# Hybrid decoder trunk: issue order of the rounded-weight and remainder products within a K tile

## What is computed

```python
def swiglu(h, w_gate, w_up, w_down):
    return (jax.nn.silu(h @ w_gate) * (h @ w_up)) @ w_down

for l in range(DEPTH):                       # DEPTH = 2
    x = x + 0.5 * swiglu(rmsnorm(x, norm_ffn1_g[l]), ffn1_w_gate[l], ffn1_w_up[l], ffn1_w_down[l])
    h = rmsnorm(x, norm_mix_g[l])
    proj = h @ w_in[l]
    q, k, v, c_b, c_c, c_u, g_attn, g_conv = jnp.split(proj, split_idx, axis=-1)
    ...
    merged = jax.nn.sigmoid(g_attn) * y_attn + jax.nn.sigmoid(g_conv) * y_conv
    x = x + merged @ w_out[l]
    x = x + 0.5 * swiglu(rmsnorm(x, norm_ffn2_g[l]), ffn2_w_gate[l], ffn2_w_up[l], ffn2_w_down[l])
return rmsnorm(x, final_g)
```

## Time and profile before

| what | value |
|---|---|
| median of three runs | 1123.29 us |
| lowest and highest | 1123.13 and 1127.27 us |
| the profiled execution's span | 1122.4 us |
| mean granted TensorE clock | 0.993 |

### The profile page before, as it was taken

How to read it: one execution, slowest core, us unless ns; L and a number is a source line. 1 busy time by engine, 2 the same in 40 slices (tenths; PEclk the granted TensorE clock), 3 DMA queues, 4 the chain that set the end, 5 groups by cost and what they waited for, 6 DMA issues and landing times.

```text
span 1122.4 us, 19933 instructions
## 1 busy us (share of the span) xinstructions
PE 1099.8 (98%) x6512; PEld 967.6 (86%) x6512; DVE 830.8 (74%) x1016; ACT 642.9 (57%) x908; POOL 20.2 (2%) x38
## 2 busy tenths in 40 slices
PE   6999999999999999999899999999999999999996
PEld 5888888888899888888788888888888998888885
DVE  5877767778898877666667776767788988676666
ACT  7655544556765655554455555445667656555454
POOL 5100000000000000000000000000000000000000
PEclk9999999999999999999989999999999999999998
DMA  8766655655555565655645656465445655656551
GB/s 218 244 188 186 196 172 177 215 163 161 170 188 170 176 198 182 192 171 176 205 133 181 202 171 194 158 209 188 150 154 183 196 175 179 195 176 199 171 188 37
DMA packets 202462, 201.76 MB, mean 180 GB/s; under 512 B 7904, under 2 KB 201472, under 8 KB 202416
## 3 DMA queue, kind: packets, MB, share of 16 engines
q1 hardware_dynamic: 200288, 199.25, 56.6%
q0 software_dynamic: 992, 1.87, 0.8%
q10 hardware_dynamic: 1136, 0.05, 0.1%
HBM read 199.32 MB, written 1.84 MB: 179 GB/s over the span
## 4 chain that ended last, share of the span: by engine, by line
PE 96%; DVE 1%; ACT 1%; DMA 1%; issue 1%; SPq 0%; DVEq 0%; ACTq 0%
PE acc L1114 57%; PE acc L1121 31%; PE acc L1118 4%; DMA raw<-in_ffn_w_gate_dram 1%; PE mixed L1118 1%; PE score L1118 1%; PE mixed L1154 0%; PE score L1222 0%; ACT w_hi L474 0%; PE mixed L1121 0%; PE score L1121 0%; PE mixed L1243 0%; PE mixed L1230 0%; PE mixed L1236 0%; ACT L508 0%
## 5 line engine op out<-in xcount | busy, mean ns | idle before, releaser
L1114 PE MATMUL acc<-xm,w_hi 128*128 128x512 f32 x2048 | 727.9, 400 | 6.9 <-issue 4.3
L1121 PE MATMUL acc<-xm,w_lo 128*128 128x256 f32 x2048 | 575.2, 281 | 0.0
L758 DVE TENSOR_TENSOR w_lo<-raw,w_hi 128x1024 fp32r<-128x1024 f32 (+1 forms) x387 | 455.6, 1199 | 147.7 <-ACT w_hi L474 146.7
L1114 PEld LDWEIGHTS acc<-xm,w_hi 128*128 128x128 f32 x2048 | 386.4, 189 | 100.9 <-issue 7.7
L474 ACT CAST w_hi<-raw 128x1024 fp32r<-128x1024 f32 (+1 forms) x387 | 389.6, 1030 | 132.7 <-PE acc L1121 120.6
L1121 PEld LDWEIGHTS acc<-xm,w_lo 128*128 128x128 f32 x2048 | 388.3, 190 | 0.2
L1121 PE MATMUL acc<-hm,w_lo 128*128 128x256 f32 x896 | 251.4, 281 | 0.0
L1114 PE MATMUL acc<-hm,w_hi 128*128 128x512 f32 x704 | 247.8, 397 | 0.0
L1121 PEld LDWEIGHTS acc<-hm,w_lo 128*128 128x128 f32 x896 | 169.7, 189 | 0.0
L486 ACT COPY acc_lo<-acc 128x512 f32<-128x512 f32 x144 | 84.2, 585 | 134.9 <-PE acc L1121 134.7
L1114 PEld LDWEIGHTS acc<-hm,w_hi 128*128 128x128 f32 x704 | 132.2, 188 | 32.3
(11 more groups left out here) (145 smaller groups left out, 476.7 us busy)
## 6 DMA issues: line engine op xcount, KB each, us to landing
raw<-in_ffn_w_gate_dram SPq DMA_DIRECT2D x88, 512.0 KB, 4.8
raw<-in_ffn_w_up_dram SPq DMA_DIRECT2D x88, 512.0 KB, 3.8
raw<-in_ffn_w_down_dram SPq DMA_DIRECT2D x80, 512.0 KB, 4.6
raw<-in_w_in_dram SPq DMA_DIRECT2D x80, 512.0 KB, 4.3
raw<-in_w_out_dram SPq DMA_DIRECT2D x16, 512.0 KB, 4.1
raw<-in_ffn_w_down_dram SPq DMA_DIRECT2D x16, 256.0 KB, 3.1
raw<-in_w_branch_attn_dram SPq DMA_DIRECT2D x8, 512.0 KB, 3.5
raw<-in_w_branch_conv_dram SPq DMA_DIRECT2D x8, 512.0 KB, 3.9
```

Of the source, the lines that this page charges most:

```text
L758: nc.vector.tensor_tensor(w_lo[:, s, 0:tiles, :], raw[:, s, 0:tiles, :], w_hi[:, s, 0:tiles, :], ALU.subtract).then_inc(lo_split, 1)
L1114: nc.tensor.matmul(banks[:, m, :], w_hi[:, r, k, cols], x[:, 0:2 * SEQ], start=first and k == 0, stop=False, skip_group_check=True)
L1121: mm = nc.tensor.matmul(banks[:, m, 0:SEQ], w_lo[:, r, k, cols], x[:, 0:SEQ], start=False, stop=end, skip_group_check=True)
```

## The change

Within each K tile, the loop over the two column tiles is split in two. The first loop issues the rounded-weight products of both column tiles; the second issues the remainder products of both. The matmuls, their operands, their outputs and the flag of the last one are the same.

```diff
@@ -1106,10 +1106,10 @@
 
                 r = slot[0] % RING
                 wait(pe, *needs, (hi_split, unit.now + 1), (lo_split, unit.now + 1 + RING))
+                ends = len(x_tiles) - 1
                 for k, x in enumerate(x_tiles):
                     for m in range(PAIR):
                         cols = slice(m * P, (m + 1) * P)
-                        end = last and k == len(x_tiles) - 1
                         if halves:
                             nc.tensor.matmul(banks[:, m, :], w_hi[:, r, k, cols], x[:, 0:2 * SEQ],
                                              start=first and k == 0, stop=False, skip_group_check=True)
@@ -1118,8 +1118,10 @@
                                 nc.tensor.matmul(banks[:, m, 0:SEQ], w_hi[:, r, k, cols], x[:, at_x:at_x + SEQ],
                                                  start=first and k == 0 and at_x == 0, stop=False,
                                                  skip_group_check=True)
+                    for m in range(PAIR):
+                        cols = slice(m * P, (m + 1) * P)
                         mm = nc.tensor.matmul(banks[:, m, 0:SEQ], w_lo[:, r, k, cols], x[:, 0:SEQ],
-                                              start=False, stop=end, skip_group_check=True)
+                                              start=False, stop=last and k == ends, skip_group_check=True)
                 mm.then_inc(used, 1)
                 unit.add()
                 slot[0] += 1
```

## The result

The changed kernel takes 1111.76 us (median of 4 runs, 1110.38 to 1114.09) against 1123.21 us for the kernel before (now the median of four runs, 1122.8 to 1127.27). The ratio is 0.9893, with a 95% interval from 0.9873 to 0.9913: 11.5 us less. The forecast was 5 us less.

What follows compares the result with a forecast made beforehand. TensorE, through distances between matmul starts, was taken to bound the kernel. Span 1122.4 us, 0 for parts that stay, -5 for fewer size changes gave 1117.4; with 0.9 for the median, 1118 us, range 1103 to 1134.

Steps and rivals of the forecast that it cites:

- What bounds the kernel: Whole kernel: TensorE busy 1099.8 of 1122.4 us, chain 96% on it; only distances between matmul starts can move the time.
- no wait moves: Waits around the loops and on other engines: buffers arrive as before and releasers stay, so cost zero.
- The base price: Each weight load in a K tile: 13 ns above the columns, same for both sizes; four before and after, difference 0.
- The slip: K tiles with alternating sizes: 6.7 ns extra per slow pair, about 2050 pairs, 13.7 us; a third to half goes, 5 us.
- The halving: Inside each K tile: size changes fall from four to two, taken to remove 4.5 to 7 us, rounded to 5.
- the first (nothing, spacings drawn at each entry): K tile stretches: spacing depends on how a stretch is entered, not size changes; 1109 to 1128 us, 1123 if unchanged; chance 0.34.
- The second (the load under a short stream not covered): Steps lo0 to lo1 and lo1 to hi0: second short matmul starts late; 1135 to 1146 us; chance 0.14.
- The third (bank): K tile matmuls: writing the same PSUM bank twice in succession costs 14 ns; 39 us would go, 1084 us; chance 0.06.
- The fourth: TensorE's matmul order: the engine keeps the old order, so nothing moves; no share of its own.
- The profile signs: TensorE timeline: steps 0.23, 0.23, 0.12, 0.12; K tile 0.693 to 0.700 us; over 454 L1114 matmuls from 940 to 1100 us; idle unchanged.

Runs made afterwards that it cites:

- eights: Against the kernel before, each unit issues all eight rounded-weight products, then all eight remainder products: 1113.59 us, ratio 0.9921.
- the swap: Against the kernel before, K tile order hi0 hi1 lo1 lo0: sizes in twos, bank changing only every second matmul as before; 1110.82 us, ratio 0.9905.
- the alternating run: Against the kernel before, hi0 lo1 over a unit's four K tiles, then hi1 lo0: sizes alternate, bank changes nearly always; 1121.82 us, ratio 0.9998.
- the repeated pair: The kernel before and the changed kernel, each run and profiled once more without edit: 1123.37 us (ratio 1.0003) and 1111.35 us (ratio 0.9877).
- fours: Against the kernel before, each unit issues four rounded-weight products of a column tile, its four remainders, then the other column tile: 1117.8 us, ratio 0.9954.

## Why the prediction was off

What bounds the kernel, and that no count changes: right. The chain and the counts are the same. That no wait moves: wrong at two places, the jump between the layers and, with a small effect, the norm at the start. The rest of the effect is in distances of PE.

The base price of 13 ns per load, the same in both orders: right as a sum, wrong as a picture. The four loads of a K tile stand 57 ns above the columns in the new order (697 - 640) and 53 or 66 in the old; but 13 ns isn't the same for both sizes: in eights a long step has 17 ns above its 213, a short one 12 or 13 above its 107.

The slip: that it belongs to the order of the sizes and not to the bank is borne out by the swap and the alternating run. Its size was the first failing step. I took "a third to a half" of the 13.7 us away (6.7 ns from each of 2050 pairs), 5 us in the sum. Measured, the slow pairs lost 4.9 of 6.7 ns, three quarters, and the quick ones grew by 1.8: 8.7 us by the same counts. And the share of quick pairs was read from one execution as if it were the program's; in the next one the long stretch of 30 to 206 us was slow, which adds up to 509 x 6.7 ns = 3.4 us to the gain, less what was quick elsewhere in that execution. With the units of the repeated pair set side by side, 13.0 us apart, the spacing alone gave 11.1 us. The halving had no ground in the rows: the fours and eights, with fewer changes of size than the twos, have longer K tiles (701.6 and 698.4 ns against 697), so the cost doesn't follow the number of changes, as I had it. What the slip is stays open.

The missing term, the second failing step: the layer boundary. The view of waits had the 4.3 us wait ("issue") in its second line; I passed over it as smaller than the first, and put the parts outside the K tiles at zero and PE's idle time as fixed. Its releaser said that the wait had no engine behind it. It gave 2.4 us, and the clock behind it 2.2 us, in the profiled pair; in the repeated pair the wait gave 1.5 us (3.4 to 1.9) and the clock nothing.

The rivals: the first (nothing, spacings drawn at each entry) was right on the old order, as its repetition shows, and wrong on the new one, which has one spacing. The second (the load under a short stream not covered) has its mechanism confirmed below 256 columns, but at 256 two short steps in succession cost 0.23 us, no more than the 2 x 0.12 of rows 10, so it had no price here. The third (bank) is refuted by the swap and the alternating run. The fourth is answered by the timeline: the matmuls come in twos, as written. The profile signs were right on the steps: 0.23, 0.23, 0.12, 0.12, the K tile at 0.697 in all stretches, 0.72 us a K tile with L1118. Two were not: PE's idle time fell with the wait at the jump, and the window from 940 to 1100 us holds 448 matmuls of L1114, not more than 454, because the last unit now ends near 1096 us; in the window up to 1080 us they are 402 against 398.

## What to carry to other kernels

Where matmuls follow each other without a gap, the distance between starts is the thing to read, in several stretches and in two executions: a program of alternating sizes can have two spacings that are drawn anew, and an order in twos traded them for a steady one here. Ask of each "issue" wait at a loop's jump back what it waits for before calling it fixed; a new timing of the instructions can move it. An effect that depends on such phases shouldn't be scaled by a count of events; try the neighbouring orders instead.

## What the runs showed of the hardware

Each weight load here has 128 columns of type fp32r. With 128 instead of 256 columns streaming over every second load, a pair got only 7 to 13 ns shorter where 53 ns of columns went, so such a load isn't hidden under 128 columns; by the rows at 400.37 and 400.47 us it holds the array for about 0.10 us, one reading of one place. Steps of 256 columns take 118 to 120 ns in runs of four or eight, while in twos they take 115, with long steps of 233 instead of 230 to 232 ns. Why the alternating order has a pattern at 693 and one at 706 ns, and what picks it, is open; shown is only that it differs between executions of one program, and that changing the bank more often doesn't remove the slow one.
